# Recurrent mixers of a transformer block pair: intermediate values in PSUM banks, another form of 1 − a², and a new order of the projections

## What is computed

```python
h = rmsnorm(x, norm_mix_g)
gate, xr = split(h @ w_in, 2)               # 2 x 1280 channels
gate = gelu(gate)
xr = causal_dwconv(xr, conv_w) + conv_b     # 4 taps along the tokens
r  = sigmoid(xh @ gate_a_w + gate_a_b)      # 16 heads of 80 channels, block diagonal
ig = sigmoid(xh @ gate_x_w + gate_x_b)
log_a = -8 * r * softplus(-lam)
a = exp(log_a)
u = sqrt(-expm1(2 * log_a)) * (ig * xr)     # sqrt(1 - a^2) * ...
hs[t] = a[t] * hs[t-1] + u[t]               # scan along the tokens
x = x + (hs * gate) @ w_out
```

## Time and profile before

| | |
|---|---|
| median of 3 runs | 3339.66 us (3338.02 to 3340.26) |
| the profiled execution: time | 3338.18 us |
| the profiled execution: span on the core | 3336.4 us |
| granted TensorE clock, mean | 0.964 |
| TensorE matmuls busy | 3119.6 us (94%) |
| VectorE busy | 1659.5 us (50%) |
| ScalarE busy | 695.2 us (21%) |
| GpSimd busy | 1888.4 us (57%) |

### The profile page before, as it was taken

The page is one execution under the profiler, slowest core; times in us unless marked ns, Lnnn a source line. Parts: engine busy times, 40 slices in busy tenths (PEclk is TensorE's granted clock), DMA queues, the critical chain, the costliest instruction groups (busy, mean ns, idle before and its releaser), DMA issues.

```text
span 3336.4 us, 37648 instructions
## 1 busy us (share of the span) xinstructions
PE 3119.6 (94%) x13568; PEld 2501.1 (75%) x13568; DVE 1659.5 (50%) x1941; ACT 695.2 (21%) x1170; POOL 1888.4 (57%) x1030
## 2 busy tenths in 40 slices
PE   6878799989999778999999999999999998889998
PEld 3666646868887567888878888888888886678886
DVE  7876763257652797422236422266522258852222
ACT  3245452111000323201013201110211113321110
POOL 4412204656665456666666666666666665556664
PEclk8978899999999789999999999999999999899999
DMA  6600102223222122232232222223222222222222
GB/s 242 243 30 32 32 1 89 95 76 100 97 95 95 57 76 82 95 101 95 95 101 89 95 99 97 95 95 100 92 98 95 97 96 85 77 81 97 99 95 69
DMA packets 86010, 306.69 MB, mean 92 GB/s; under 512 B 9552, under 2 KB 10064, under 8 KB 85632
## 3 DMA queue, kind: packets, MB, share of 16 engines
q1 hardware_dynamic: 82512, 297.73, 26.7%
q10 hardware_dynamic: 3376, 7.24, 0.6%
HBM read 302.84 MB, written 2.10 MB: 91 GB/s over the span
## 4 chain that ended last, share of the span: by engine, by line
PE 79%; DVE 15%; issue 3%; ACT 2%; SPq 1%; DMA 0%; DVEq 0%; ACTq 0%
PE acc L1510 74%; DVE rec_rec_x L1900 2%; DVE rec_rec_in L1929 2%; DVE rec_rec_u L1942 1%; PE side L724 1%; DVE ada_more L1098 1%; PE acc L702 1%; DVE state L1244 1%; SPq L494 0%; DMA xc<-in_ctx 0%; DVE rec_rec_in L1927 0%; DVE rec_rec_u L1931 0%; DVE rec_rec_x L1896 0%; PE acc L628 0%; DVE rec_rec_in L1893 0%
## 5 line engine op out<-in xcount | busy, mean ns | idle before, releaser
L1473 POOL TENSOR_TENSOR w_lo<-w_raw,w_hi 128x1024 fp32r<-128x1024 f32 x513 | 1241.6, 2420 | 1380.3 <-PE acc L1510 1333.2
L1510 PE MATMUL acc<-h_hi,w_hi 128*128 128x512 f32 x2224 | 884.2, 398 | 72.1 <-DVE rec_rec_in L1893 17.4
L1510 PE MATMUL acc<-h_lo,w_hi 128*128 128x512 f32 x2224 | 874.4, 393 | 0.0
L1510 PE MATMUL acc<-h_hi,w_lo 128*128 128x512 f32 x2224 | 873.7, 393 | 0.0
L1463 POOL TENSOR_SCALAR w_hi<-w_raw 128x1024 fp32r<-128x1024 f32 x513 | 663.9, 1294 | 36.4 <-DMA w_raw<-in_weights 36.4
L1510 PEld LDWEIGHTS acc<-h_hi,w_hi 128*128 128x128 f32 x2224 | 422.3, 190 | 180.4 <-issue 18.3
L1510 PEld LDWEIGHTS acc<-h_hi,w_lo 128*128 128x128 f32 x2224 | 422.5, 190 | 86.8
L1510 PEld LDWEIGHTS acc<-h_lo,w_hi 128*128 128x128 f32 x2224 | 423.3, 190 | 85.0 <-issue 2.0
L1862 DVE TENSOR_TENSOR x<-acc,x 128x512 f32 (+1 forms) x160 | 110.7, 692 | 610.3 <-PE acc L1510 610.1
L1510 PE MATMUL acc<-mlp_hid_hi,w_hi 128*128 128x512 f32 x1024 | 398.3, 389 | 0.0
L1510 PE MATMUL acc<-mlp_hid_lo,w_hi 128*128 128x512 f32 x1024 | 398.3, 389 | 0.0
(11 more groups left out here) (320 smaller groups left out, 3623.9 us busy)
## 6 DMA issues: line engine op xcount, KB each, us to landing
w_raw<-in_weights SPq DMA_DIRECT2D x513, 512.0 KB, 3.3
ada<-in_ada SPq DMA_DIRECT2D x36, 512.0 KB, 5.6
ada_more<-in_ada SPq DMA_DIRECT2D x10, 512.0 KB, 17.7
x<-in_x ACTq DMA_DIRECT2D x16, 256.0 KB, 6.6
out<-x SPq DMA_DIRECT2D x8, 256.0 KB, 2.2
cvec<-in_cvec ACTq DMA_DIRECT2D x1, 1024.0 KB, 5.8
ada_n<-in_ada SPq DMA_DIRECT2D x2, 512.0 KB, 16.8
xc<-in_ctx SPq DMA_DIRECT2D x1, 1024.0 KB, 16.3
```

The costliest lines, as they stand in the source:

```text
L1473: pool.tensor_tensor(w_lo[:, slot, :], w_raw[:, slot, :], w_hi[:, slot, :].bitcast(F32), ALU.subtract).then_inc(panel_made, 1)
L1510: ins = pe.matmul(out, lhs, rhs, start=start, stop=stop, skip_group_check=group)
```

## The change

- **Conv and gates stay in PSUM.** The x projection is scaled in its bank, the first three taps read the bank and write `rec_x` in SBUF, and the last tap writes the bank again. Taps are shifted in the output, so that no padded input buffer is needed; a three-column instruction fills the head of `rec_x` with the bias. ScalarE reads the bank twice (a copy to `rec_x` and the high part), and the bank is free only after VectorE's low part. The sigmoid of the x gate is made in its bank; the bank is free after the product with `rec_x`. The output gate is scaled in its bank, gelu is in place, the product with the scan result is in place, and the bank is free after the low part.
- **1 − a².** ScalarE makes tanh(z) and a² = exp(−16 …), and one VectorE instruction makes (a² + 1)·tanh(z). The add, the reciprocal and the multiply go.
- **Scan input** lies in the three `side` banks, in `stat` and, for the fifth tile, in SBUF.
- **Order.** TensorE: x of half 0, gates of half 0, x of half 1, gates of half 1, then all 10 output-gate projections, then down. VectorE does the scans of half 0 between the gate products of half 1.
- **Softplus of lambda** for both mixers is made once, on ScalarE behind the loads of x in the first block (after `head_high`, ahead of the branch merge), and scaled on VectorE after the merge.

```diff
+    def rec_x_out(inst, m): return first_out["mix", 3 * inst] + m + 2 * HALF * (m // HALF)
+    def rec_y_out(inst, m): return first_out["mix", 3 * inst] + 6 * HALF + m
...
 TensorE
                     skip_to_panel()
-                    for m in range(HALF):
-                        project(h_parts)
+                for m in range(RT):
+                    project(h_parts)
                 down_in_two([(M["rec_hi"][:, k, :], M["rec_lo"][:, k, :]) for k in range(RT)],
-                            lambda k: pe.wait_ge(rec_lo_made, rec_y_lo(inst, k)))
+                            lambda k: wait_taken(pe, rec_y_out(inst, k)))
...
 ScalarE, in the first block
             for k in range(KT):
                 act.dma_start(x[:, k, :], io["x"][:, k, :]).then_inc(x_in, 16)
+            act.activation(rec_cl[:, 0, :], table[:, ...], ACT.Exp, scale=-1.0).then_inc(rec_cl_exp, 1)
+            act.wait_ge(rec_cl_exp, 1)
+            act.activation(rec_cl[:, 1, :], rec_cl[:, 0, :], ACT.Ln, bias=col("one")).then_inc(rec_cl_ln, 1)
...
 ScalarE
+                def conv_high(o, m):
+                    act.wait_ge(rec_conv, RT * inst + m + 1)
+                    act.activation(M["rec_x"][:, m, :], bank(o), ACT.Copy)
+                    act.activation(M["rec_hi"][:, m, :], bank(o), ACT.Copy).then_inc(rec_hi_made, 1)
+                def decays(done, gate_o):
+                    for i in range(HALF + 1):
+                        if i < HALF:
...
+                            if i == 0 and done:
+                                act.wait_ge(rec_scan, done)
+                            if i >= 4:
+                                act.wait_ge(rec_ratio, done + i - 3)
+                            act.activation(M["rec_u"][:, i, :], a, ACT.Tanh, ...)
+                            act.activation(M["rec_sq"][:, i % 4, :], a, ACT.Exp, ...)
+                        if i:
...
+                            act.activation(a, a, ACT.Exp, ...)     # tile i - 1
...
+                for i in range(HALF): gates(o + 2 * i, i)
+                decays(first, o)
+                conv_high(o, HALF); roots(first, range(0, 3))
+                conv_high(o + 1, HALF + 1); roots(first, range(3, HALF))
+                for i in range(2, HALF): conv_high(o + i, HALF + i)
+                for i in range(HALF): gates(o + 2 * i, HALF + i)
+                decays(first + HALF, o)
+                gelu(o, 0); gelu(o + 1, 1); y_high(o, 0); y_high(o + 1, 1)
+                roots(first + HALF, range(HALF))
+                gelu(o + 2, 2)
+                for m in range(3, RT + 1):
+                    if m < RT: gelu(o + m, m)
+                    y_high(o + m - 1, m - 1)
...
 VectorE
+                def convolved(o, m):
+                    xr, acc_ = bank(o), M["rec_x"][:, m, :]
+                    scaled_bank(o, rec_tap)                        # bank = bank * rstd
+                    dve.tensor_scalar(acc_[:, 0:3], ones[:, 0:3], col("a_conv_b", first + m), None, ALU.mult)
+                    for j in range(A_TAPS - 1):
+                        back = A_TAPS - 1 - j
...                     # j = 0: tensor_scalar, else scalar_tensor_tensor: bank -> acc_[:, back:]
+                    dve.scalar_tensor_tensor(out=xr, in0=xr, scalar=w[3], in1=acc_, op0=ALU.mult, op1=ALU.add)
+                def low(o, m, hi_count):
+                    dve.wait_ge(rec_hi_made, hi_count)
+                    dve.tensor_tensor(M["rec_lo"][:, m, :], bank(o), M["rec_hi"][:, m, :], ALU.subtract) # frees bank
+                def ratio(done, i):
+                    dve.scalar_tensor_tensor(out=M["rec_u"][:, i, :], in0=M["rec_sq"][:, i % 4, :], scalar=1.0,
+                                             in1=M["rec_u"][:, i, :], op0=ALU.add, op1=ALU.mult)
+                def scanned(done, i, gate_o):
+                    dve.tensor_tensor(s_at[i], s_at[i], M["rec_x"][:, m, :], ALU.mult)
+                    dve.tensor_tensor_scan(M["rec_x"][:, m, :], M["rec_a"][:, m, :], s_at[i], 0.0, ALU.mult, ALU.add)
+                for m in range(HALF + 1):                          # half 0
+                    if m < HALF: convolved(o + m, m)
+                    if m: conv_low(o + m - 1, m - 1)
+                for i in range(HALF): inner(o + 2 * i + 1, i)      # half 0
+                convolved(o, HALF)
+                for i in range(HALF): ratio(first, i)
+                conv_low(o, HALF)
...                     # half 1: convolved(6), convolved(7), conv_low(6), ... conv_low(9)
+                for i in range(HALF): inner(o + 2 * i + 1, HALF + i); scanned(first, i, gates[0])
+                ratio 0, 1; scaled_bank(o); ratio 2, 3; scaled_bank(o + 1); ratio 4
+                gated(o), gated(o + 1); y_low(o), y_low(o + 1); scaled_bank(o + 2)
+                scanned 0, 1; scaled_bank(o + 3); scanned 2, 3, 4
+                for m in range(2, RT): gated(o + m); scaled_bank(o + m + 2) if m + 2 < RT; y_low(o + m)
...
 weights on the host
-                for m in ms:
-                    out.append(packed(panels_by_column(w_in, 0, KT, m)))
+            for m in range(RT):
+                out.append(packed(panels_by_column(w_in, 0, KT, m)))
```

More of the change, by code:

```diff
@@ L1335, in first_block_dve @@
                 own(dve.tensor_tensor(mg_lo[:, m, :], gm, mg_hi[:, m, :].bitcast(F32), ALU.subtract), mg_lo_made, m + 1)
+            dve.wait_ge(rec_cl_ln, 1)
+            for i, scale in ((0, -16.0), (2, 8.0), (3, -8.0)):
+                dve.tensor_scalar(rec_cl[:, i, :], rec_cl[:, 1, :], scale, None, ALU.mult).then_inc(rec_cl_made, 1)
             dve.wait_ge(x_in, 16 * 2 * KT)
@@ new lines, in roots, with gelu, y_high @@
+                def roots(done, part):
+                    for i in part:
+                        act.wait_ge(rec_ratio, done + i + 1)
+                        act.activation(s_at[i], M["rec_u"][:, i, :], ACT.Sqrt).then_inc(rec_sqrt, 1)
+                def gelu(o, m):
+                    act.wait_ge(rec_gated, RT * inst + m + 1)
+                    act.activation(bank(o), bank(o), ACT.Gelu_apprx_tanh).then_inc(rec_gelu, 1)
+                def y_high(o, m):
+                    act.wait_ge(rec_y, RT * inst + m + 1)
+                    act.activation(M["rec_hi"][:, m, :], bank(o), ACT.Copy).then_inc(rec_hi_made, 1)
@@ new lines, in recurrent @@
+                norm_root(norm)
+                first = RT * inst
+                for m in range(HALF):
+                    conv_high(o + m, m)
+                o += HALF
+                act.wait_ge(rec_cl_made, 3)
+                for i in range(HALF):
+                    gates(o + 2 * i, i)
+                decays(first, o)
+                o += 2 * HALF
+                conv_high(o, HALF)
+                roots(first, range(0, 3))
+                conv_high(o + 1, HALF + 1)
+                roots(first, range(3, HALF))
@@ new lines, in recurrent @@
+                for i in range(2, HALF):
+                    conv_high(o + i, HALF + i)
+                o += HALF
+                for i in range(HALF):
+                    gates(o + 2 * i, HALF + i)
+                decays(first + HALF, o)
+                o += 2 * HALF
+                gelu(o, 0)
+                gelu(o + 1, 1)
+                y_high(o, 0)
+                y_high(o + 1, 1)
+                roots(first + HALF, range(HALF))
+                gelu(o + 2, 2)
+                for m in range(3, RT + 1):
+                    if m < RT:
+                        gelu(o + m, m)
+                    y_high(o + m - 1, m - 1)
@@ new lines, in gated, with y_low @@
+                def gated(o, m):
+                    dve.wait_ge(rec_gelu, first + m + 1)
+                    dve.wait_ge(rec_scan, first + m + 1)
+                    dve.tensor_tensor(bank(o), bank(o), M["rec_x"][:, m, :], ALU.mult).then_inc(rec_y, 1)
+                def y_low(o, m):
+                    low(o, m, 2 * first + RT + m + 1)
+                for m in range(HALF + 1):
+                    if m < HALF:
+                        convolved(o + m, m)
+                    if m:
+                        conv_low(o + m - 1, m - 1)
@@ new lines, in recurrent @@
+                o += HALF
+                gates = [o, o + 3 * HALF]
+                for i in range(HALF):
+                    inner(o + 2 * i + 1, i)
+                o += 2 * HALF
+                convolved(o, HALF)
+                for i in range(HALF):
+                    ratio(first, i)
+                conv_low(o, HALF)
+                for i in range(1, HALF + 1):
+                    if i < HALF:
+                        convolved(o + i, HALF + i)
+                    if i > 1:
+                        conv_low(o + i - 1, HALF + i - 1)
@@ new lines, in recurrent @@
+                o += HALF
+                for i in range(HALF):
+                    inner(o + 2 * i + 1, HALF + i)
+                    scanned(first, i, gates[0])
+                o += 2 * HALF
+                ratio(first + HALF, 0)
+                ratio(first + HALF, 1)
```

(20 more changed lines are left out.)

199 lines of the change are left out of this document (71 added, 128 removed).

## The result

The changed kernel takes 3293.43 us (3291.95 to 3295.66), the kernel before, on the same chip, 3338.84 us (3337.97 to 3340.26): ratio 0.9864, 95% interval 0.9848 to 0.988. That is 45 us where 70 were forecast, and 1.4 us outside the range. The profiled execution spans 3290.2 us against 3336.4.

A forecast was written before the change was run, and what follows sets the result against it. TensorE was taken as the bound, losing 95.2 us in two mixers; 22.8 would remain, gaining 72.4. With 1.9 lost in the merge, 3338.2 became 3267.7 us, or 3269 for the median; range 3248 to 3292.

The forecast's parts named there:

- The wait ahead of down: TensorE's 10.9 us wait before the mixer's down projection; claimed to vanish, with inputs there when down starts.
- the three places: TensorE pauses per mixer: third gate output of each half (2.3, 2.4 us) and sixth or seventh output-gate projection.
- The tail: From the end of the second half's gates: TensorE idle 0.8 us for a bank, plus 1.2 for scans, 2.0 us.
- The merge: Softplus of lambda ahead of the first sigmoid in the first block's merge: 1.9 us lost, bounds 0 and 3.7.
- the first step: Pricing VectorE's instructions in the mixers: fill 0.08 us, conv step with low part 4.6, ratio 0.75 for most.
- the ratio: VectorE's one scalar_tensor_tensor per tile: 0.75 us for most, plus one 0.8 us delay per half.
- the walk through the order: Timing of the second mixer through both halves and tail: 7.5 us idle plus 3.9 for restarts, 11.4 left per mixer.
- bound of 6 us for a pause: Upper bound on each TensorE pause in the mixers; bounds 0 and 6 us give 3246 to 3290 us.
- the second step: Whole-kernel sum: 3338.2 less 72.4 in the mixers plus 1.9 in the merge, 3267.7 us; no other terms.
- The second, bank turnover binds: Mixers: each pause doubles through unpriced waits, scans and ratios meet GpSimd each time; 3297 us, chance 0.15.
- The third, the clock: Mixers: TensorE pauses for banks again and again, so its clock stays low; about 3381 us, chance 0.03.
- The fourth: Mixers: little changes, conv steps stay at 6.85 us or above because GpSimd holds them; 3320 us, chance 0.05.

The follow-up runs named there:

- e3: Changed kernel with the three-column fill reading the tap's PSUM bank instead of a constant in SBUF: 3272.77 us, ratio 0.9796 to the kernel before.
- e7: Changed kernel with both the fill reading the tap's PSUM bank and a*a written to PSUM: 3273.82 us, ratio 0.9805 to the kernel before.
- E4: Changed kernel with ScalarE's a*a written into a PSUM bank for four of five tiles of a half: 3281.61 us, ratio 0.9834 to the kernel before.
- E5: Changed kernel with 192 bytes per partition of padding behind rec_cl, moving the hidden and recurrent tiles: 3285.09 us, ratio 0.9840 to the kernel before.
- e11: Kernel before with only the 1 − a² formula changed; order, conv, gates and buffers as before: 3337.88 us, ratio 0.9995.
- e12: Changed kernel with only the formula undone (add, reciprocal and multiply back, no second exp): 3365.90 us, ratio 1.0085 to the kernel before.

## Why the prediction was right and wrong

**Right.** TensorE's loss in the mixers was what could be won. The wait ahead of down is gone; no panel was waited for; taps stand at 0.75 and 0.76 us, the first at 0.80, the scan from a bank at 1.22. Banks are the new coupling, and pauses stand at the three places. The tail was forecast at 2.0 us and is 1.95 and 1.89. The table loads are 1.28 us again. Of the 2.66 us that the Trainium skill gives for a switch of tables ("ScalarE: Activation LUTs", "What ACT_TABLE_LOAD costs"), the load is seen in this case's traces and the drain is not: in the mixers the activation behind a load starts 0.01 us after it.

**Right by luck.** The merge was priced at 1.9 us, with bounds of 0 and 3.7. Where it stands it costs 3.4: the changed kernel is 0.9 us ahead at the matmul at 522.71 before and 2.4 behind at that at 546.57, by a pause of 1.83 us and the low clock behind it. The same matmul of the first mixer then comes 1.97 us late (1114.72 against 1112.75), but that agreement says little: in e3 and e7, whose first block is the same, it comes at 1118.06 and 1115.52.

**Wrong, the first step.** "The three-column fill 0.08, an estimate", and for the ratio "I take 0.75 for most and 0.8 us for one delay per half". The fill took 0.78 on average and 2.37 at most, the ratio 1.67 and 2.90. E3 shows what the fill did, by changing the operand and not the work: a long fill is a fill on SBUF alone that began inside a GpSimd instruction and ended with it. E4 does so for the ratio: with one input in a bank it takes 0.69 us inside a GpSimd instruction too. The prediction had the cause in hand. It priced the taps by it, and took the bound between 0.75 and 2.85 for the ratio from the earlier trace rows. But it looked at the size of the fill and not at its operands, and put the ratio at the lower bound although GpSimd is busy for 57% of the span. The Trainium skill, page "SBUF — State Buffer", section "SBUF: two separate sides", has this as a rule: VectorE and GpSimd share a pair of ports, and a GpSimd instruction, or a VectorE instruction that has two inputs in SBUF or runs in a two-port mode, takes them from its start to its end, while the other engine's waits in full. This case's trace agrees: 1167.93 and 1167.96. The ratio has two SBUF inputs. Which of the two conditions the fill meets, no run here shows. For the mixers it is 38.7 us lost against 22.8 forecast; with the fill mended 18.9 are lost in the two, with both mended 9.9 and 9.7. So the fill alone is the term whose mending closes the gap (20.7 us in e3); the ratio alone gives 11.8 (e4), but nothing more once the fill is mended. So the walk through the order (11.4 left) was right to 1.7 us a mixer, and the pauses with both mended are 1.9, 2.5 and 1.9 us where it said 2.3, 2.4 and 2.0. Its bound of 6 us for a pause was passed by the middle ones, 7.2 and 7.6 us together.

**Wrong, the second step.** The sum had no term for it: a new 320-byte tile moves every stage's tiles. "Other parts of the program are bound by matmuls one behind the other" was right, and so each of 3,072 hidden matmuls carried the price. E5 takes 8.3 us off the time, and its trace shows them where they were lost: from the first MLP's first matmul to the one at which the count of the second mixer begins it is 1378.3 us before, 1384.8 in the changed kernel and 1379.7 in e5.

**The size** comes out of these: 15.9 us in the mixers and 8.4 in the unchanged stages are the 24.3 by which the profiled gain, 46.2, stays under 70.5. Without either of the two the time would lie inside the range.

**The rivals.** The second, bank turnover binds at 3297 us, is nearest in time and half right: pauses did grow because VectorE met GpSimd. But the first grew by the fills, which it did not name (3.76 us with the ratio mended in e4, 1.94 with the fill mended in e3), and the middle one by fills and ratios together. The scans from a bank did not meet it (1.22 us, all sixteen; the four with both inputs in SBUF took 1.95), and the tail was as forecast. The third, the clock: it fell twice in each mixer (mean 0.98 and 0.97 over the mixers), and did not stay low. The fourth: that the conv steps are still held (3320 us) was true of one instruction in six.

**The parts.** The formula is worth nothing in the old order (e11) and 72.5 us in the new one (e12); without it the new order and the banks are slower than the kernel before. The prediction had priced the edits as one walk, which is why it got the direction. Order and banks apart from each other were not tried.

## What to carry to other kernels

Before pricing a small VectorE instruction, look at its operands: if all lie in SBUF and GpSimd is busy, its bound is GpSimd's longest instruction, not its own size; with one input in PSUM it did not wait in any of the 36 cases of e3 and e4. A new SBUF tile is padded so that operands of the matmuls keep their offsets within 256 bytes, or goes behind the others (not tried here); a line without computation was worth 8 us here, and another one cost 45. Removing work from an engine gained nothing while its next input came at a fixed pace (e11): change the order first, then see which instruction binds.
